# A decoder step: the last projected tile looped by pairs of k, cache gathers issued from within it, and the last norms' root taken ahead of ScalarE's counts

## What is computed

```python
def att_project(h, w_in, g_q, g_k):
    q, k, v, qi, ki, wi = jnp.split(h @ w_in, ATT_SPLITS, axis=-1)
    q = rms_norm(q.reshape(B, T, N_KV_HEADS, GROUP, HEAD_DIM), g_q)
    k = rms_norm(k.reshape(B, T, N_KV_HEADS, HEAD_DIM), g_k)
...
def dsa_block(q, qi, wi, q_pos, k_all, v_all, ki_all, topk):
    logits = jnp.einsum('bqhd,bsd->bqhs', qi, ki_all)
    score = jnp.einsum('bqh,bqhs->bqs', wi, jax.nn.relu(logits)) * IDX_SCALE
    score = jnp.where(admissible[None], score, -jnp.inf)
    _, sel = lax.top_k(score, topk)
    ...
    p = jax.nn.softmax(s, axis=-1)
    o = jnp.einsum('bqhgk,bqkhd->bqhgd', p, v_sel)
```

## Time and profile before

| | us |
|---|---|
| median of 3 runs | 2774.66 (2774.5 to 2779.32) |
| profiled execution | 2789.16 |
| its span, first to last instruction | 2787.4 |
| TensorE busy in it | 2678.9 |
| VectorE, ScalarE, GpSimd busy | 1404.3, 861.9, 108.8 |

### The profile page before, as it was taken

How to read it: one execution, slowest core, us unless ns; L and a number is a source line. 1 busy time by engine, 2 the same in 40 slices (tenths; PEclk the granted TensorE clock), 3 DMA queues, 4 the chain that set the end, 5 groups by cost and what they waited for, 6 DMA issues and landing times. The chain is left out here.

```text
span 2787.4 us, 44801 instructions
## 1 busy us (share of the span) xinstructions
PE 2678.9 (96%) x17409; PEld 2561.6 (92%) x17458; DVE 1404.3 (50%) x2742; ACT 861.9 (31%) x1492; POOL 108.8 (4%) x137
## 2 busy tenths in 40 slices
PE   8899888899999999999999989999999999999997
PEld 7799756677899999999999989989999999999997
DVE  6567776775434444444444454342544444444444
ACT  5577586574222111111111141230411111111110
POOL 1300123100000000000000000000000000000000
PEclk9899999999999999999999999999999999999999
DMA  5313389600111111111111111111111111111111
GB/s 193 92 34 99 136 330 384 259 1 1 39 38 41 43 45 45 45 45 44 39 45 45 46 31 46 39 34 45 38 46 45 40 43 45 45 45 45 45 40 69
DMA packets 182108, 197.43 MB, mean 71 GB/s; under 512 B 14312, under 2 KB 154858, under 8 KB 173805
## 3 DMA queue, kind: packets, MB, share of 16 engines
q1 hardware_dynamic: 170141, 120.40, 14.3%
q0 software_dynamic: 11776, 75.50, 7.2%
q10 hardware_dynamic: 80, 0.02, 0.0%
HBM read 184.17 MB, written 11.73 MB: 70 GB/s over the span
## 5 line engine op out<-in xcount | busy, mean ns | idle before, releaser
L579 DVE TENSOR_TENSOR trunk_xT<-ffn_acc,trunk_xT 128x364 f32<-128x364 f32 x528 | 272.8, 533 | 162.9 <-PE ffn_acc L647 162.7
L647 PE MATMUL ffn_acc<-ffn_act_hi,trunk_w_hi 128*128 128x364 f32 (+1 forms) x1056 | 345.7, 327 | 3.5 <-DVE ffn_act_lo L545 3.5
L647 PE MATMUL ffn_acc<-ffn_act_lo,trunk_w_hi 128*128 128x364 f32 (+1 forms) x1056 | 347.4, 329 | 0.0
L647 PE MATMUL ffn_acc<-ffn_act_hi,trunk_w_lo 128*128 128x364 f32 (+1 forms) x1056 | 345.5, 327 | 0.0
L635 PE MATMUL ffn_acc<-ffn1x_x_hi,trunk_w_hi 128*128 128x364 f32 (+1 forms) x1032 | 338.4, 328 | 1.2 <-DVE ffn_norm_tmp L553 1.2
L635 PE MATMUL ffn_acc<-ffn0x_x_hi,trunk_w_hi 128*128 128x364 f32 (+1 forms) x1032 | 338.4, 328 | 1.2 <-DVE ffn_norm_tmp L553 1.2
L635 PE MATMUL ffn_acc<-ffn1x_x_hi,trunk_w_lo 128*128 128x364 f32 (+1 forms) x1032 | 338.4, 328 | 0.0
L635 PE MATMUL ffn_acc<-ffn0x_x_hi,trunk_w_lo 128*128 128x364 f32 (+1 forms) x1032 | 338.3, 328 | 0.0
L635 PE MATMUL ffn_acc<-ffn1x_x_lo,trunk_w_hi 128*128 128x364 f32 (+1 forms) x1032 | 338.0, 328 | 0.0
L635 PE MATMUL ffn_acc<-ffn0x_x_lo,trunk_w_hi 128*128 128x364 f32 (+1 forms) x1032 | 338.0, 327 | 0.0
L494 ACT ACTIVATE trunk_w_hi<-trunk_w_raw 128x1024 fp32r<-128x1024 f32 x130 | 136.7, 1051 | 415.1 <-PE ffn_acc L647 415.1
(11 more groups left out here) (446 smaller groups left out, 5070.4 us busy)
## 6 DMA issues: line engine op xcount, KB each, us to landing
trunk_w_raw<-in_ffn_w_gu SPq DMA_DIRECT2D x88, 512.0 KB, 3.9
trunk_w_raw<-in_ffn_w_down SPq DMA_DIRECT2D x44, 512.0 KB, 3.7
trunk_w_raw<-in_sg_w_in SPq DMA_DIRECT2D x16, 512.0 KB, 3.9
attxm_w_raw<-in_att_w_in SPq DMA_DIRECT2D x14, 512.0 KB, 5.9
search_row_buf<-r_kept SPq DMA_DIRECT2D x10, 512.0 KB, 4.4
x_kept<-x_xT SPq DMA_DIRECT2D x8, 544.0 KB
trunk_xT<-x_kept SPq DMA_DIRECT2D x8, 544.0 KB, 7.9
att_proj<-in_x_prompt SPq DMA_DIRECT2D x8, 512.0 KB, 6.8
```

Source lines behind the costliest of these rows:

```text
L579: nc.vector.tensor_tensor(xT[:, o, a:a + w], banks[e % 6][:, 0:w], xT[:, o, a:a + w], ALU.add).then_inc(drained, 1)
L647: last = nc.tensor.matmul(banks[e % 6][:, 0:w], part[:, t * 512 + o * P:t * 512 + (o + 1) * P], (a_hi, a_lo)[m][:, t, a:a + w], start=(t = ...
```

## The change

Four parts. (1) The last tile's loop on TensorE: k outside, in four pairs from the highest down (`K_PAIRS` = 3, 2, 1, 0), the three chunks inside; a new semaphore, `pair_used`, counts the first three pairs. `turn_r` of the last pair of norms comes after the first pair of k, the value transposes after the second and the third. (2) The ring's slots are laid so that each lies within one pair's part of x_hi or x_lo (`OWN_ORDER`, `OWN_PAIR` = 3, 3, 2, 2, 1, 0), and GpSimd issues a gather once the pair below it has been used: two after the first pair, two after the second, one after the third, one after the last product. (3) On ScalarE the last root comes before its two counts; on VectorE the last tile's drains all come at the end, behind the last two norms. (4) The second search's rounds are hosted one by each bank of sample attention, 0 to 31, where three ran before bank 0 and banks 8, 16 and 24 had none.

```diff
             pool.wait_ge(spread_ready, 2 * PAIRS)
-            pool.wait_ge(products, NC3 * COUNT)
             for u in range(OWN):
+                i = K_PAIRS.index(OWN_PAIR[u])
+                if i < len(K_PAIRS) - 1:
+                    pool.wait_ge(pair_used, i + 1)
+                else:
+                    pool.wait_ge(products, NC3 * COUNT)
                 ring.gather(pool, u)
...
-            for m in range(COUNT):
+            def last_tile():
+                m = COUNT - 1
+                s = (m + IDX_TILES) % 2
+                pe.wait_ge(weights.lo_ready, m + IDX_TILES)
+                for i, p in enumerate(K_PAIRS):
+                    for k in (2 * p, 2 * p + 1):
+                        first, final = i == 0 and k == 2 * p, i == len(K_PAIRS) - 1 and k == 2 * p + 1
+                        for c, (a, w) in enumerate(CHUNKS):
+                            if first:
+                                pe.wait_ge(evacuated, NC3 * (m - 2) + c + 1)
+                            for j, (part, x) in enumerate(W.parts(s)):
+                                last = nc.tensor.matmul(banks[NC3 * (m % 2) + c][:, 0:w], part[:, k * P:(k + 1) * P],
+                                                        x_parts[x][:, k, a:a + w], start=(first and j == 0),
+                                                        stop=(final and j == 2))
+                            if final and c < NC3 - 1:
+                                last.then_inc(products, 1)
+                    if i < len(K_PAIRS) - 1:
+                        last.then_inc(pair_used, 1)
+                        at = 3 * m + i
+                        if at in R_AT:
+                            turn_r(R_AT[at])
+                        if at in V_AT:
+                            wait_copied("v", V_AT[at])
+                            turn_v(0, V_AT[at], tr)
+                    else:
+                        last.then_inc(products, 1)
+
+            for m in range(COUNT - 1):
...
-                if j == 0 and m % 2 == 1 and m >= 3:
+                if j == 0 and m % 2 == 1 and 3 <= m < COUNT - 1:
                     R.scalar(nc, act, (m - 3) // 2)
...
                 if at_ == ROUNDS:
                     act.wait_ge(exact, 1)
                     swap()
+                    R.scalar(nc, act, HEADS // 2 - 1)
...
-                    drain(m, 0)
+                    if m < COUNT - 1:
+                        drain(m, 0)
...
-                    drain(m, 1)
+                    if m < COUNT - 1:
+                        drain(m, 1)
...
-            drain(COUNT - 1, 2)
             norm(HEADS - 2)
             norm(HEADS - 1)
+            for c in range(NC3):
+                drain(COUNT - 1, c)
...
-OWN = 6
+SLOT = 2 * TOK
+OWN_HI, OWN = KT // 2, 6
+K_PAIRS = tuple(range(KT // 2 - 1, -1, -1))
...
-        own = self.own = S.sb("ring", [P, OWN, UW], side="right")
-        self.slot = [own[:, j, :] for j in range(OWN)] + [spare[:, j * UW:(j + 1) * UW] for j in range(RING - OWN)]
+        hi = S.sb("ring_hi", [P, OWN_HI, SLOT], side="right")
+        lo = S.sb("ring_lo", [P, SLOT + UW], side="right")
+        over = [hi[:, j, 0:UW] for j in range(OWN_HI)] + [lo[:, j * UW:(j + 1) * UW] for j in range(OWN - OWN_HI)]
+        self.slot = [over[j] for j in OWN_ORDER] + [spare[:, j * UW:(j + 1) * UW] for j in range(RING - OWN)]
...
-    hosts = [-1, -1, -1] + [S for S in range(BANKS) if S < STEPS or S % STEPS]
+    hosts = list(range(BANKS))
```

More of the change, by code:

```diff
@@ L1849, in search_stage @@
             S.sem(n) for n in ("above", "at", "above_counted", "crossed", "tail", "selected", "sp_zero"))
-        spread_ready = S.sem("spread_ready")
+        spread_ready, pair_used = S.sem("spread_ready"), S.sem("pair_used")
         block = S.block(no_gpsimd_drain=True)
@@ L1959, in _ @@
                         turn_r(R_AT[at])
-                    if at in V_AT:
-                        wait_copied("v", V_AT[at])
-                        turn_v(0, V_AT[at], tr)
+            last_tile()
             pe.wait_ge(R.link, R.LINKS * (HEADS // 2 - 1) + 1)
@@ L2408 @@
 UW = UK * NKV * HD
-OWN = 6
+SLOT = 2 * TOK
+OWN_HI, OWN = KT // 2, 6
+K_PAIRS = tuple(range(KT // 2 - 1, -1, -1))
+OWN_ORDER = tuple(x for p in K_PAIRS for x in ([p] + ([OWN_HI + p - (KT // 2 - (OWN - OWN_HI))] if p >= KT // 2 - (OWN - OWN_HI) else [])))
+OWN_PAIR = tuple(p for p in K_PAIRS for _ in range(1 + (p >= KT // 2 - (OWN - OWN_HI))))
 RING = OWN + (NPROJ - VTILE) * TOK // UW
@@ L2838, in trunk @@
                 with Scope(nc, "held") as K:
-                    K.sb("rest_of_x_and_w", [P, 2 * KT * TOK + 6 * D + TOK - OWN * UW], side="right")
+                    K.sb("rest_of_x_and_w", [P, 2 * KT * TOK + 6 * D + TOK - OWN_HI * SLOT - SLOT - UW], side="right")
                     search_stage(nc, proj, a["att_q_norm"][0], a["att_k_norm"][0], W, weights, x_parts, rows, v_nat, k_outs,
```

## The result

The new kernel takes 2784.27 us (median of 10 runs), the one before beside it 2776.42 us; the ratio is 1.0026, 95% interval 1.0018 to 1.0035. By the medians it is 7.9 us slower, by the ratio 7.2 (5.0 to 9.7), where 2775.3 with 2770.5 to 2779.5 had been forecast. A second set of runs gave 1.0034 (1.0021 to 1.0048).

The account below looks back on a forecast made before the run. TensorE, busy 96% of the span, was taken to bound the kernel. The terms +1.05 - 3.2 + 1.75 + 1.0 gave +0.6 us on 2774.66, so 2775.3 us, range 2770.5 to 2779.5.

Parts of the forecast that it names:

- The root ahead of the counts: Last tile, ScalarE: the earlier root leaves 0.9 of TensorE's 3.05 us wait before the reciprocals' transpose; VectorE's scan starts earlier.
- The wait in the tile: Last tile: TensorE stands still 3.4 us before the second value transposes; the next stage starts +1.05 or -0.4 us.
- the clock falls behind it: TensorE's clock drops after the 3.4 us wait, giving +1.05 us; the rival that it stays up had chance 0.22.
- The row loads: End of search stage: loads for VectorE's last two norms run beside four early gathers; 0 to +0.8 us, taken as 0.
- So 0 to +0.8 us, taken as 0: Cost of the last norms' row loads running beside early gathers; ScalarE's last copies cover VectorE until rows at 328.2.
- sharing evenly: Row loads sharing the DMA engines evenly with the gathers would land at about 325.5.
- slow down but aren't last: Row loads interleave with gathers on the DMA engines, so their term stays 0; by strict order it would be 0.8.
- The start of sample attention: Five of six first slots are full, so TensorE's waits of 5.67 and 1.80 us shrink or go: -3.2 us.
- The bound of 5: Start of sample attention: gain up to 5 us if sixteen transposes without a pause bring the clock back early.
- The moved rounds: Search rounds moved to banks 8, 16 and 24 of sample attention: +1.75 us for the first, +1.0 for the others.
- The two later places: Rounds moved to banks 16 and 24: 0 to 2.5 us each, taken as 0.5 each, +1.0 together.
- The rival on the slower side: The rounds decide: key copies in all three host banks wait 2.5 us each; +6.5, 2781.2 us, chance 0.13.

Follow-up runs that it names:

- rows_first: The new kernel with GpSimd's first gather held until both rows of the last pair of norms have landed; 2774.1 us, ratio 0.9995 to the kernel before.
- hold_gathers: The new kernel with all six gathers held until the last product of the last tile, as before; ratio 1.0012 to the kernel before.
- two_early: The new kernel with two gathers issued early and the other four held until both rows have landed; 2773.6 us, ratio 0.9997 to the kernel before.
- old_hosts: The new kernel with search rounds hosted as before: three ahead of bank 0, none in banks 8, 16, 24; 2788.3 us, ratio 1.0042 to the kernel before.
- before_again: The kernel before, unchanged, as a second profiled execution; ratio 1.0004 to the kernel before.
- the first profile: The profiled execution of the unchanged kernel before that the prediction read; it took 2789.16 us.
- hosts_only: The kernel before with one search round in each bank and none ahead of bank 0; ratio 1.0001 to the kernel before.
- after_again: The new kernel, unchanged, as a second profiled execution; ratio 1.0034 to the kernel before.

## Why the prediction was wrong, step by step

**The root ahead of the counts: right.** A wait of 0.9 us was forecast in place of 3.05; it is 0.70. The scan starts 6.0 us into the tile (312.05), 6.1 forecast.

**The wait in the tile: right, its price partly.** 3.4 us forecast, 3.33 measured. That the clock falls behind it was taken as the likelier case. In the new kernel's own two profiles it doesn't (last matmul at 17.2, and 17.2 had been worked out for a clock that stays up), nor in rows_first. In hold_gathers, two_early and old_hosts it does, and then the last matmul comes at 19.7, not 18.6 as worked out. The reason given, that the wait is longer than the one of 3.05 us that lowered the clock, fails: a wait of 3.04 us left it up in before_again. What decides this can't be told from these runs.

**The row loads: the step that failed.** "So 0 to +0.8 us, taken as 0". It is 6.7 us against hold_gathers and 9.3 against rows_first, and 3.7 more in the second execution. The first of these is the smaller because hold_gathers, with its clock down, reached the boundary late for another reason; rows_first had the clock up like the new kernel, so 9.3 is the fair price. Three things were wrong in the step. The small store ahead of the loads was moved with them and not costed: it shares the engines too, and SyncE waits for its landing (5.69 us instead of 1.24). The rows were taken to be last at worst behind four gathers, near 329 in the time of the first profile, or 17.5 us into the tile; the second was complete 24.9 us into the tile, 10.7 us after the fifth gather's issue (14.2). And sharing evenly was taken as the middle case. The last 32 KB of the second row, issued at 319.16, took 11.7 us to land, as long as the whole gathers of 1.05 MB issued around them (10.9 us for the one of 317.71, 11.0 for the one of 320.23). So a small transfer beside gathers got no quick passage for being small.

Why is open. The DMA rows show 603 packets for 1.12 MB from SyncE's queue and 864 for 6.29 MB from GpSimd's, 1.9 KB a packet against 7.3. If the engines took turns by packet, rows would get about a fifth (1.9 of 9.2) of the 430 GB/s, 89 GB/s, and their 1.05 MB would take 11.8 us; from the first row load's issue to the second norm it was 13.2. That is an estimate, not shown by a run: no experiment changed the size of a packet, and loads that simply stand behind most of what was queued before them would be late as well. The Trainium skill, "DMA: Bandwidth & Descriptors", section "Queues, rings and completion order", says that an engine goes round its queues packet by packet, in which a packet there is a bundle of descriptors and need not be what the profile counts. The prediction's "slow down but aren't last" held by a hair: the rows were complete at 330.9, the fifth gather at 331.2. Its error was to take the slowing as nothing.

**The start of sample attention: right in sign, too small.** -3.2 us forecast. From the stage's start to the 17th gather it takes 36.6 us instead of 42.7, so -6.0. The bound of 5 was meant for an early clock and that came: the third group of eight transposes took 1.32 us (341.56 in the rows above), where in the kernel before it took 1.97. But the mechanism was only half of it. With the slots just as full and the three rounds back ahead of bank 0 (old_hosts) the stretch takes 42.7 us, no less than before: TensorE then waits for ScalarE's key copies. With the rounds moved and the slots empty (hosts_only) it takes 39.6. So full slots alone gave nothing by the 17th gather, the moved rounds alone gave 3.1 us, and both together 6.0. The prediction counted the moved rounds as a cost only.

**The moved rounds: the size was off.** +1.75 for bank 8; measured 3.6 (11.8 instead of 8.2 us). ScalarE's copies of bank 10 are late by 1.7 us as forecast:

```profile
371.38 0.94 ACT L1170 ACTIVATE satt_early_hit<-masks_Sp,masks_level 128x768 bf16<-128x768 f32 x1 [0.93 <-DVE masks_level L1186]
...
378.86 1.54 ACT L2702 ACTIVATE satt_KT<-satt_tr 128x512 f32<-128x512 f32 x3
```

(7.5 us from round to copies; before 5.8, from 373.56 to 379.31.) The other 1.9 us arise in the banks after. The two later places were taken at +1.0 and cost nothing measurable in hosts_only.

**The sum by the measured terms,** against before_again: +10.0 at the boundary, -6.0 to the 17th gather, +3.0 to the 20th (18.0 us instead of 15.0), -0.6 from there to prompt attention: +6.3, and the time moved by +7.9 by the medians, +7.2 (5.0 to 9.7) by the ratio. That they agree so well is in part luck: against the first profile, whose sample attention happened to take 4.1 us longer, the same sum is +1.1. The forecast sum was +1.05, -3.2, +1.75, +1.0. So behind the boundary the forecast was 3 us too dear (-0.45, measured -3.6), which hid part of the 9 us missed at the boundary. The base of the forecast, 2774.66, was a median of three runs; ten gave 2776.42, which makes 1.8 of the 9.0 us between 2775.3 and 2784.27. The rival on the slower side named the rounds as the mechanism and gave 2781.2; it was slower, but for another reason. Three rounds in the banks gained 4 us here (old_hosts against the new kernel).

## What to carry to other kernels

A prefetch that is moved earlier takes the DMA engines from whatever else is in flight there. Before moving it, list the small transfers in its new time, each store that is waited for and each load that hangs on it, and put the prefetch behind those that VectorE or TensorE needs first: the order cost 9 us here (9.3 at the boundary, 8.6 by the ratios) and one wait gave them back. When a wait is removed from an engine's order, look for the next instruction on that engine that has to wait for the same tail.

## What the runs showed of the hardware

From the issue of a 9 KB store to the next instruction, which waits for its landing, it took 1.24 us with nothing else in flight, 5.33 us with two gathers of 1.05 MB queued ahead of it (two_early), and 5.69, 7.12 and 5.00 us with a third issued beside it (the new kernel's two executions and old_hosts). Row loads of 0.5 MB, which landed in 3.0 to 5.0 us by themselves, took up to 12.8 us beside gathers, and their companions of 32 KB up to 14.1.

GpSimd's issue of a gather, 0.94 to 0.99 us for the other four of the new kernel's six and up to 1.9 elsewhere, took 4.02 and 2.21 us while VectorE ran its scan (312.05) and the two operations behind it. The same was seen in after_again and old_hosts (4.01 and 2.21); its cause wasn't tested.

A wait of 3.3 us on TensorE between dense matmuls left the granted clock at full in three executions (the new kernel's two, rows_first) and lowered it in three others (hold_gathers, old_hosts, two_early). One of 3.03 to 3.05 us lowered it in one execution of three.
